# One-hots of the gate stage's columns in bf16, two early expert blocks fewer, and another order of stores in a fused attention, pooling and PEER layer

## The reference

```python
q = (h @ peer_wq).reshape(B, T, 8, 256)          # 8 heads
s1, s2 = q1 . sub_keys1, q2 . sub_keys2          # 128 scores each
v1, i1 = top_k(s1, 16); v2, i2 = top_k(s2, 16)
top_s, pos = top_k(v1[i] + v2[j], 16)            # 16 experts a head
eid = i1 * 128 + i2 at pos; gate = softmax(top_s)
a = gelu(einsum('td,tkd->tk', h, peer_u[eid]))
out = einsum('tk,tkd->td', gate * a, peer_v[eid])
```

## Time and profile before

| what | value |
|---|---|
| median of three runs | 960.62 us |
| profiled execution | 962.64 us |
| span of its trace | 960.8 us |
| PE busy | 950.7 us (99%) |
| DVE busy | 765.0 us (80%) |
| ACT busy | 476.5 us (50%) |
| POOL busy | 210.0 us (22%) |
| DMA | 174.72 MB, mean 182 GB/s |
| PE clock granted | full throughout |

### The profile page before, as it was taken

The page is one execution under the profiler, slowest core; times in us unless marked ns, Lnnn a source line. Parts: engine busy times, 40 slices in busy tenths (PEclk is TensorE's granted clock), DMA queues, the critical chain, the costliest instruction groups (busy, mean ns, idle before and its releaser), DMA issues.

```text
span 960.8 us, 16339 instructions
## 1 busy us (share of the span) xinstructions
PE 950.7 (99%) x5324; PEld 827.5 (86%) x5324; DVE 765.0 (80%) x1454; ACT 476.5 (50%) x846; POOL 210.0 (22%) x249
## 2 busy tenths in 40 slices
PE   9999999999999999999999999999999999999998
PEld 9998899898888888888888888888888888888887
DVE  5899759899999998888676776777777777777776
ACT  6576554433888874334334434434444444444442
POOL 3075238887777740000000000000000000000000
PEclk9999999999999999999999999999999999999999
DMA  9544138826443458777555555555555555555554
GB/s 289 155 132 132 45 109 292 214 57 208 147 130 118 137 178 264 241 236 237 176 190 202 175 196 197 178 197 192 179 202 187 179 206 183 181 210 177 187 206 153
DMA packets 73593, 174.72 MB, mean 182 GB/s; under 512 B 6208, under 2 KB 39104, under 8 KB 73296
## 3 DMA queue, kind: packets, MB, share of 16 engines
q1 hardware_dynamic: 73120, 172.02, 53.4%
q0 software_dynamic: 288, 2.10, 1.1%
q10 hardware_dynamic: 144, 0.08, 0.0%
HBM read 165.26 MB, written 6.82 MB: 179 GB/s over the span
## 4 chain that ended last, share of the span: by engine, by line
PE 77%; DVE 1%; issue 0%; ACT 0%; DVEq 0%; ACTq 0%
PE psum L1964 36%; PE psum L1944 17%; PE psum L1829 10%; PE psum L1947 9%; PE psum L1907 3%; PE psum L1529 0%; DVE big L1329 0%; DVE big L1123 0%; DVE big L1119 0%; DVE big L1158 0%; DVE big L1150 0%; DVE big L1131 0%; PE psum L1895 0%; ACT gel L689 0%; DVE big L1147 0%
## 5 line engine op out<-in xcount | busy, mean ns | idle before, releaser
L1964 PE MATMUL psum<-rr 128*128 128x512 f32 x1536 | 366.0, 391 | 0.1
L1964 PEld LDWEIGHTS psum<-rr 128*128 128x128 f32 x1536 | 287.4, 188 | 60.0 <-issue 0.2
L1944 PE MATMUL psum<-h_all,rr 128*128 128x512 f32 x728 | 260.6, 392 | 0.0
L785 ACT ACTIVATE rr<-raw 128x1024 fp32r<-128x1024 f32 x94 | 99.7, 1061 | 235.5 <-PE psum L1964 234.5
L1247 DVE TENSOR_TENSOR rr<-raw,rr 128x1024 fp32r<-128x1024 f32 x94 | 115.2, 1225 | 123.1 <-ACT rr L785 123.1
L1947 PE MATMUL psum<-h_all,rr 128*128 128x256 f32 x728 | 188.7, 280 | 0.0
L1944 PEld LDWEIGHTS psum<-h_all,rr 128*128 128x128 f32 x728 | 136.6, 188 | 27.2 <-DVE rr L1163 0.3
L1947 PEld LDWEIGHTS psum<-h_all,rr 128*128 128x128 f32 x728 | 136.7, 188 | 7.1
L1829 PE MATMUL psum<-t32s,raw 128*128 128x256 f32 x576 | 131.8, 379 | 1.5 <-ACT gel L689 1.0
L683 ACT ACTIVATE rr<-raw 128x1024 fp32r<-128x1024 f32 x91 | 96.6, 1062 | 50.2 <-DMA raw<-in_peer_u_dram 48.7
L1829 PEld LDWEIGHTS psum<-t32s,raw 128*128 128x128 f32 x576 | 106.1, 190 | 15.0 <-issue 1.6
(11 more groups left out here) (213 smaller groups left out, 1137.4 us busy)
## 6 DMA issues: line engine op xcount, KB each, us to landing
raw<-in_peer_v_dram SPq DMA_DIRECT2D x128, 512.0 KB, 3.6
raw<-in_peer_u_dram SPq DMA_DIRECT2D x127, 512.0 KB, 4.0
big<-in_w_in_dram SPq DMA_DIRECT2D x10, 1024.0 KB, 5.4
big<-in_peer_wq_dram SPq DMA_DIRECT2D x8, 1024.0 KB, 6.9
up_kept<-gel SPq DMA_DIRECT2D x36, 128.0 KB, 2.1
gel<-up_kept SPq DMA_DIRECT2D x34, 128.0 KB, 4.0
big<-in_w_out_dram SPq DMA_DIRECT2D x4, 1024.0 KB, 5.4
rr<-big POOLq DMA_DIRECT2D x2, 1024.0 KB, 11.5
```

Of the source, the lines that this page charges most:

```text
L785: act.activation(v_sp[s][:, 0, :], v_raw[s], ACT.Copy).then_inc(v_hi, 1)
L1944: return pe.matmul(both, ut[s][:, 0, k, :], ht[:, :, k, :], start=(k == 0), stop=(k == DK - 1))
L1964: i = pe.matmul(psum[:, 4 + 2 * t + n, :], g_sp[:, s, x, t * P:(t + 1) * P], v_sp[s][:, y, n * 512:(n + 1) * 512], start=(first and m == 0 ...
```

## The change

1. `EARLY` goes from 36 to 34 and `EARLY_TOP` from 14 to 15. So blocks 0 to 13 run ahead of the gate stage, blocks 14 to 33 in it (20 in place of 23), and blocks 34 and 35 are computed later with split parts. `RING_END` goes from 34 to 31.
2. The numbers 0 to 127 stand in PSUM as bf16, each repeated eight times (`numbers_in`). ACT writes them into SBUF as bf16 and copies the bits to PSUM as 512 fp32 words.
3. The column picks are kept as bf16 (`pick16`), and `cols` is bf16 with the token innermost: `[number, token]` in place of `[token, number]`. So ACT and POOL now read `cols` with a step of eight elements (16 bytes). `rows_at` stays fp32r and is made from `numbers_in` read with the same step.
4. The copy of the picks on ACT becomes two.
5. `keep_early(e)` stores the Gelu of block `e - 1` rather than `e`, behind the ring's load.
6. The residual rows are stored after `keep_early(0)`, and `WQ0+7` is loaded after `keep_early(2)`. The last blocks' loads of values no longer wait for the gate stage's multiplications, since `cols` takes half the space.

```diff
-EARLY, EARLY_TOP = 36, 14
+EARLY, EARLY_TOP = 34, 15
...
-        cols = raw[:, 2 * D:4 * D].rearrange("p (s q n) -> p s q n", s=2, q=GRP)
+        cols = raw[:, 3 * D:4 * D].bitcast(BF16).rearrange("p (s n q) -> p s n q", s=2, q=GRP)
+        pick16 = picks[:, 1, 0:SEQ // 2].bitcast(BF16)
+        numbers_sb = big[:, xs_at:xs_at + NK * GRP // 2]
...
-        iota_in = psum[:, 0, 0:NK]
+        numbers_in = psum[:, 0, :].bitcast(BF16).rearrange("p (n q) -> p n q", q=GRP)
...
-            sp.wait_ge(h_ev, 2 * N_OUT)
-            for t in range(2):
-                sp.dma_start(h_dram[t], xt[:, t, :]).then_inc(st_h, 16)
...
+            def store_early(e):
+                sp.wait_ge(e_gel, e + 1)
+                sp.dma_start(up_dram[e], gel[:, e % 2, :]).then_inc(st_e[e % 2], 16)
             def keep_early(e):
                 sp.wait_ge(e_up, e + 1)
                 if e + 3 < EARLY:
                     load_ring(e + 3)
-                elif e == EARLY - 3:
+                if e:
+                    store_early(e - 1)
+                if e == EARLY - 3:
...
-                    sp.wait_ge(ohg_up, NQ - 1)
-                    sp.wait_ge(ohp_up, NQ - 1)
...
-                sp.wait_ge(e_gel, e + 1)
-                sp.dma_start(up_dram[e], gel[:, e % 2, :]).then_inc(st_e[e % 2], 16)
...
                 keep_early(e)
-                if e == 1:
+                if e == 0:
+                    sp.wait_ge(h_ev, 2 * N_OUT)
+                    for t in range(2):
+                        sp.dma_start(h_dram[t], xt[:, t, :]).then_inc(st_h, 16)
+                if e == 2:
                     load_w(WQ0 + 7)
...
             numbers(PH - 1)
+            act.activation(numbers_sb.bitcast(BF16).rearrange("p (n q) -> p n q", q=GRP), iota.unsqueeze(2).to_broadcast([P, NK, GRP]),
+                           ACT.Copy).then_inc(a_iota, 1)
             for e in range(PH - 2, EARLY_TOP - 3):
                 early_gelu(e)
-            act.activation(iota_in, iota, ACT.Copy).then_inc(a_iota, 1)
+            act.wait_ge(a_iota, 1)
+            act.activation(psum[:, 0, :], numbers_sb, ACT.Copy).then_inc(a_iota, 1)
...
-                        i = act.activation(pairs_at[q % 2][:, j, part, :], cols[:, q % 2, j, :], ACT.Copy, scale=scale)
+                        i = act.activation(pairs_at[q % 2][:, j, part, :], cols[:, q % 2, :, j], ACT.Copy, scale=scale)
...
-            def ones(out, a, tok, n):
-                dve.tensor_tensor(out, iota_in.unsqueeze(1).to_broadcast([P, n, NK]),
-                                  picks[:, a, tok:tok + n].unsqueeze(2).to_broadcast([P, n, NK]), ALU.is_equal).then_inc(oh_up, 1)
+            def ones_cols(q):
+                dve.tensor_tensor(cols[:, q % 2], numbers_in, pick16[:, GRP * q:GRP * (q + 1)].unsqueeze(1).to_broadcast([P, NK, GRP]),
+                                  ALU.is_equal).then_inc(oh_up, 1)
+            def ones_rows(q):
+                dve.tensor_tensor(rows_at[q % RS], numbers_in.rearrange("p n q -> p q n"),
+                                  picks[:, 0, GRP * q:GRP * (q + 1)].unsqueeze(2).to_broadcast([P, GRP, NK]), ALU.is_equal).then_inc(oh_up, 1)
```

More of the change, by code:

```diff
@@ L746, in _ @@
             act.wait_ge(pe_pk, 1)
[L747 removed]
+            act.activation(pick16, psum[:, 6, SEQ:2 * SEQ], ACT.Copy).then_inc(pk_ev, 1)
+            act.activation(picks[:, 0, :], psum[:, 6, 0:SEQ], ACT.Copy).then_inc(pk_ev, 1)
             act.wait_ge(pe_pk, 2)
@@ L1230, in _ @@
                     dve.wait_ge(ohp_up, q - 1)
-                ones(cols[:, q % 2], 1, GRP * q, GRP)
+                ones_cols(q)
                 if q == 0:
-                    dve.wait_ge(pk_ev, 2)
+                    dve.wait_ge(pk_ev, 3)
                     dve.tensor_tensor(picks[:, 2, :].rearrange("p (a k m) -> p a k m", a=2, k=DK),
```

15 lines of the change are left out of this document (8 added, 7 removed).

## The result

The changed kernel takes 989.2 us (median of four runs, 986.11 to 992.95) against 960.53 us for the kernel before: a ratio of 1.0292, 95% interval 1.0266 to 1.0319. The forecast was 957.4, with a range of 954 to 975. The changed kernel's profiled execution took 986.74 us (span 985.0).

The account below looks back on a forecast made before the run. DVE was taken to set the gate stage's pace, PE 0.1 us a group behind. Terms -1.33 (blocks), -2.0 (PE waits), +1.06 (copy), -1.0 (SP's order) gave -3.3 us: 957.4 us measured, range 954 to 975.

Parts of the forecast that it names:

- Behind the stage: After the gate stage: blocks 34 and 35 become late ones, each 5.52 us in place of 2.75, +5.54.
- Ahead of the stage: Before the first gate matmul: one more early block +3.50 us, ACT's new copy +1.06, SP's order -1.0.
- Gate stage: Three early blocks leaving take 10.37 us of PE, hidden PE waits fall by 2.0; the stage takes 95.5 us.
- I leave PE 0.04 a group: Gate stage: PE at 3.01 us a group is longest and waits only 0.04 more, 1.2 us in all.
- For ACT I take the lower bound: Gate stage: ACT's products stay at 0.293 us despite the stepped read, its group at 2.91 us.
- The upper bound: ACT's stepped read, priced from DVE's 64-byte step: 0.085 us a product, 0.51 a group, so 3.42 us.
- rival 1: ACT's stepped reading costs: 3.5 us a group, gate stage 109.5 us, 971.4 in all; chance 0.15.
- the ring: ACT's loop in the gate stage: second gate half, copy, six products, next second half, about 2.96 us with hops.
- Rival 2: POOL's stepped reading costs more, 1.9 us each: gate stage 118.8 us, 980.7 in all; chance 0.10.
- Rival 3: DVE's bf16 one-hot stays at 1.13 us with a PSUM source: gate stage 108.2, 970.1 in all; chance 0.08.
- Rival 4: `WQ0+7` lands at 193.2 us, DVE's ranking 2.2 late: 960.6 in all, no change; chance 0.10.
- SP's order: Ahead of the gate stage: SP's reordered stores and loads let DVE's ranking come 1.0 us earlier.

Follow-up runs that it names:

- e3_both_dense: The changed kernel with ACT and POOL both reading `cols` side by side (wrong gates): 965.1 us, ratio 1.0041 to the kernel before.
- the pairs kernel: The changed kernel with bf16 one-hots as token pairs, 36 blocks and fourteen, Gelu of block 6 earlier: 960.91 us; with `WQ0+7` back behind block 1, 957.72.
- e9_gelu_first: The kernel before with the change's SP order, and ACT taking the Gelu of block 6 ahead of the last head's numbers: 961.56 us, ratio 1.002.

## Why the prediction was wrong

Its terms against the profiled executions, with 960.8 and 985.0 us of span:

- *Behind the stage* +5.54: measured +6.3. Right in kind; 0.5 of the rest is a wait at 479 us for a load of `u`.
- *Ahead of the stage*, +3.50 for the block, +1.06 for the copy, -1.0 for the order, together +3.6: measured +2.3, with runs of one order spreading by more than the difference. The copy did stand before the Gelus, 1.04 us long, and PE's gap grew from 1.00 to 1.39. The last head's numbers came 1.9 us earlier (216.75 for 218.67) in place of 1.0, since `WQ0+7` landed after 8.3 us, where 10 was taken.
- *Gate stage* -12.4 (-10.37 and -2.0): measured +15.7. This is the failed step, and it failed in two places of one sentence, "I leave PE 0.04 a group".

First, the price of ACT's stepped read, which the forecast put at nothing ("For ACT I take the lower bound"). It was 0.127 us a product (0.42 from start to start for 0.293), so 0.76 a group and 20.9 of the 28.1 us by which the stage missed. The argument was that over half of a product is fixed cost which may hide a slower stream. The runs show no such cover: 0.127 us more are seen at every product. The upper bound, 0.085 us from DVE's row with a step of 64 bytes, was too low as well: DVE pays 0.66 ns an element there, ACT 1.0. Bounds taken from another engine were no bounds. By its own words the forecast stood on the wrong side of a point only 0.02 us a product away, and that alone should have moved weight to rival 1.

Second, the ring. It was seen, and summed as 2.96 us with 0.72 for half of the gate matmuls and two hops. The 0.48 in it for four matmuls is half of eight that run on; the profiles have 0.78 from the start of four to ACT's read of their sum, with 0.15 ahead of it, so 0.93. So the ring is 3.18 us by its hops even with dense reads, above PE's 3.01, and the stage 99.98 us in e3_both_dense in place of 95.5. By the same hops the kernel before had it too, under DVE's 3.46. With it, -10.37 for the blocks that leave the stage could not be had in full: PE had ceased to be what bounds it. Without the steps the change would be at 962.0 to 963.0 in an undisturbed run, no gain either.

Of the rivals, 1 named the mechanism and the place, and said 971.4 where it was 989.2; with 0.127 and 0.93 in place of its numbers it gives 3.94 a group, 31 x 3.94 + 0.95 = 123.1 us, where 123.7 was measured. Rival 2 (POOL) has a real cost, 0.30 us an instruction, but behind ACT's it counts for 0.7 us, and 2.8 once ACT's is gone (with these 2.8 and the ring's 4.5, the 28.1 are complete). The forecast's 1.49 for it stands at 1.56. Rival 3 fell: 1024 elements of bf16 from PSUM took 680 ns, 0.60 from start to start, where 0.62 was forecast. "VectorE: DVE Perf Modes" of the Trainium skill, § The perf-mode tier table, has one element a cycle there, and the measurement decides against it, for the same page's text on PSUM operands with 16 bits. Rival 4, the late landing of `WQ0+7`, was seen in two profiles with that load behind block 2 (11.2 and 12.1 us) and is dearer than forecast: 5 us a run, since a lower granted clock follows PE's gap. It may be what sets two of the changed kernel's four runs (991.67 and 992.95) above the other two (986.11 and 986.74), but no profile of those was taken. The median is 28.7 us over and the profiled execution 24.1: 2.5 of the difference are these two runs, and 2.1 are the profiled execution of before, which lies above its median.

*SP's order* at -1.0: the kernels with it whose load landed in time reached block 8 at 216.6 to 217.6 us, less 1.06 for the copy where they have it, and those with the order of before at 217.7 to 219.4, so about a microsecond may be there in an undisturbed run, though the two ranges nearly touch; over all runs, with `WQ0+7` behind block 1, it is nothing (0.9999, 0.999 to 1.0008). "The stores behind ring loads cost nothing" held for PE: ACT waits for them (five times, 3.8 us at most) but PE does not. What stays open: why the late `u` load held the pairs kernel up at 463 us with one position of `WQ0+7` and not with the other, and whether the upper heap of e9_gelu_first is the same wait moved to the transposes. So the slow gate stage is explained by runs from both sides, and the spread of the runs only in part.

## What to carry to other kernels

When a layout is changed to make its writer fast, price its readers first, in bytes between neighbouring elements, and on the engine that stands in a ring of waits before the one that has room. Sum such a ring hop by hop from the starts of one group, because the second-longest thing is what a gain on the longest ends at: here three lay within 0.3 us of each other, and work may only be moved out of PE's way where PE is the longest. A load that is moved behind others needs its slack from the worst landing, not the middle one, and a median of several runs hides it if only a third of them pay.
